# Hyena filter's spectrum computed ahead of the first feed-forward, and five modulation tiles multiplied by PE

## The reference

```python
mod = c_act @ w_ada[l] + b_ada[l]                   # nine vectors of 1024
(sh1, sc1, ga1, ...) = jnp.split(mod, N_MOD, axis=-1)
h = modulate(rms_norm(x, g_pre_ff1[l]), sh1, sc1)   # needs sh1 and sc1
f = swiglu(h, w1_gate[l], w1_up[l], w1_down[l])     # the first feed-forward
...
def hyena_filter_spectra(t, z, ...):                # for the fifth stage
    h = jnp.sin(sin_freq[0] * (z @ w1 + b1))
    h = jnp.sin(sin_freq[1] * (h @ w2 + b2))
    h = jnp.sin(sin_freq[2] * (h @ w3 + b3))
    h = (h @ w_out).reshape(L, HYENA_ORDER, 2, HYENA_WIDTH)
    h = h * jnp.exp(-t[:, None, None, None] * jnp.abs(decay))
    fwd, bwd = h[:, :, 0], h[:, :, 1]
    two = jnp.concatenate([fwd, zeros, bwd[:0:-1]], axis=0)
    two = two * lax.rsqrt(jnp.sum(two * two, axis=0, keepdims=True))
    return jnp.fft.rfft(two, axis=0)
```

## Time and profile before

| | us |
|---|---|
| median of 3 runs | 1576.78 (1573.79 to 1578.28) |
| the profiled execution | 1575.49 |
| its span | 1573.7 |
| PE busy | 1524.4 (97%) |
| DVE busy | 1023.6 (65%) |
| ACT busy | 758.5 (48%) |
| POOL busy | 222.7 (14%) |

### The profile page before, as it was taken

The page is one execution under the profiler, slowest core; times in us unless marked ns, Lnnn a source line. Parts: engine busy times, 40 slices in busy tenths (PEclk is TensorE's granted clock), DMA queues, the critical chain, the costliest instruction groups (busy, mean ns, idle before and its releaser), DMA issues.

```text
span 1573.7 us, 28410 instructions
## 1 busy us (share of the span) xinstructions
PE 1524.4 (97%) x10512; PEld 1401.8 (89%) x10512; DVE 1023.6 (65%) x1391; ACT 758.5 (48%) x1205; POOL 222.7 (14%) x255
## 2 busy tenths in 40 slices
PE   5989999999999998999999999999999999999997
PEld 5989999989988888999997899999999999899996
DVE  6998778766665456655567765556655569565554
ACT  2444645576456345444454344445444457454442
POOL 1596095311001011000000000000000000000000
PEclk9999999999999999999999999999999999999999
DMA  9888874236665455655543365554655544255551
GB/s 349 320 299 279 315 266 130 79 108 199 203 224 186 168 188 209 225 189 175 196 132 96 110 227 170 194 185 136 212 188 189 174 156 137 68 200 191 171 198 40
DMA packets 80563, 294.35 MB, mean 187 GB/s; under 512 B 9051, under 2 KB 9404, under 8 KB 79916
## 3 DMA queue, kind: packets, MB, share of 16 engines
q1 hardware_dynamic: 75728, 274.97, 50.8%
q0 software_dynamic: 3984, 16.21, 3.1%
q10 hardware_dynamic: 780, 2.18, 0.5%
HBM read 289.13 MB, written 3.15 MB: 186 GB/s over the span
## 4 chain that ended last, share of the span: by engine, by line
PE 84%; DVE 8%; ACT 3%; issue 2%; DMA 1%; POOL 1%; SPq 0%; DVEq 0%; ACTq 0%
PE bank L207 74%; DVE w_lo L191 3%; DVE arena L843 2%; PE bank L431 1%; PE bank L2033 1%; PE bank L2022 1%; PE bank L1273 1%; DMA arena<-ada 1%; PE bank L2409 1%; PE bank L2387 1%; ACT arena L308 1%; PE bank L424 1%; ACT w_hi L185 0%; PE bank L1259 0%; POOL stat L349 0%
## 5 line engine op out<-in xcount | busy, mean ns | idle before, releaser
L207 PE MATMUL bank<-h_hi,w_hi 128*128 128x256 f32 x2344 | 674.4, 288 | 5.8 <-DVE w_lo L191 4.4
L207 PE MATMUL bank<-h_lo,w_hi 128*128 128x256 f32 x2344 | 664.7, 284 | 0.0
L207 PE MATMUL bank<-h_hi,w_lo 128*128 128x256 f32 x2344 | 664.5, 283 | 0.0
L191 DVE TENSOR_TENSOR w_lo<-raw,w_hi 128x1024 fp32r<-128x1024 f32 x454 | 548.4, 1257 | 109.0 <-ACT w_hi L185 108.3
L185 ACT ACTIVATE w_hi<-raw 128x1024 fp32r<-128x1024 f32 x458 | 457.9, 1050 | 55.0 <-DMA raw<-panels 28.8
L207 PEld LDWEIGHTS bank<-h_hi,w_hi 128*128 128x128 f32 x2344 | 450.7, 192 | 21.0 <-issue 6.8
L207 PEld LDWEIGHTS bank<-h_lo,w_hi 128*128 128x128 f32 x2344 | 450.9, 192 | 5.7 <-issue 1.9
L207 PEld LDWEIGHTS bank<-h_hi,w_lo 128*128 128x128 f32 x2344 | 450.7, 192 | 0.0
L668 DVE TENSOR_TENSOR arena<-arena,bank 128x256 f32<-128x256 f32 x132 | 55.3, 419 | 253.7 <-PE bank L207 180.7
L207 PE MATMUL bank<-w_hi,f_hi 128*128 128x512 f32 x528 | 207.8, 394 | 1.6 <-DVE f_lo L673 1.4
L207 PE MATMUL bank<-w_hi,f_lo 128*128 128x512 f32 x528 | 206.9, 392 | 0.0
(11 more groups left out here) (329 smaller groups left out, 1387.2 us busy)
## 6 DMA issues: line engine op xcount, KB each, us to landing
raw<-panels SPq DMA_DIRECT2D x458, 512.0 KB, 4.6
arena<-ada SPq DMA_DIRECT2D x64, 512.0 KB, 5.2
arena<-ada POOLq DMA_DIRECT2D x8, 512.0 KB, 3.9
arena<-rows POOLq DMA_DIRECT2D x4, 512.0 KB, 4.6
spectrum<-arena POOLq DMA_DIRECT2D x2, 1024.0 KB, 7.9
arena<-spectrum POOLq DMA_DIRECT2D x1, 2048.0 KB, 18.0
X<-x_in SPq DMA_DIRECT2D x1, 1024.0 KB, 6.7
arena<-decay ACTq DMA_DIRECT2D x2, 512.0 KB, 5.6
```

The lines of the kernel that those rows point to most:

```text
L191: dve.tensor_tensor(w_lo[:, slot, :], raw[:, slot, :], w_hi[:, slot, :].bitcast(F32), ALU.subtract).then_inc(lo_ready, 1)
L207: last = pe.matmul(out_ap, a, b, start=start and n == 0, stop=stop and n == 2)
```

## The change

The spectrum's work leaves the second feed-forward. All three layers, the taps of both orders and the transform of order 0 go ahead of the first feed-forward, between the modulation's tiles. The transform of order 1 goes behind the first product of the first feed-forward (tile 0), and its sum behind `up(1)`; both sit in PE's list, and ACT's evictions of that transform sit between panels 2 and 3. Its five loads are issued by ACT's queue as soon as the small columns have landed, before ACT computes silu(c). Of the 16 modulation tiles PE multiplies 1, 3, 5, 9 and 11 (`ada_tile_pe`, one matmul per column block into bank 3, on top of which `ada_first_pe` adds DVE's sums), and SP waits for them by a semaphore of their own. The two `keep_busy` runs shrink from 24 and 10 matmuls to 6 and 10. POOL's list takes the even parts and squares ahead of `ada_middle_pool`, and the stores behind it; it waits for the stores' landing before `tables_pool`. Some buffers and PSUM banks move.

```diff
@@ -545,8 +548,15 @@
                     down(2, i)
 
             norm_pe(pe, at, first_up)
+            if n == 0:
+                for f in range(2):
+                    spectrum_rows_pe(pe, 1, f)
             up(1)
+            if n == 0:
+                filter_sums_pe(pe, 1)
             down(0, start=True)
+            if n == 0:
+                pe.wait_ge(filter_sums, 2)
             if n == 0:
...
@@ -573,8 +583,6 @@
                 for f in range(2, FT - 2):
                     up(f)
                     down(f - 1)
-                    piece_pe(pe, f)
-                pe.wait_ge(filter_sums, 2)
                 gate_pe(pe, 2, acc_gate_2, (6, 7))
...
                     act_panels(act, base + 3 * f + 2, 3)
-                    piece_first_act(act, f - 1)
                     hidden(f)
-                    piece_act(act, order, f - 1)
...
@@ -692,6 +696,7 @@
             dve_panels(dve, base + 5, 3)
             if n == 0:
                 params_rest_dve(dve, order)
+                filter_sums_dve(dve, 1)
             hidden(1)
...
                     dve_panels(dve, base + 3 * f + 2, 3)
-                    piece_dve(dve, order, f - 1)
...
         def ada_add(dve, a, dst):
 
             slot, k = a % ADA_RING, a % KT
+            tiles = 2 if a + 1 in BY_PE else 1
             dve.wait_ge(ada_loaded[slot], 16 * (a // ADA_RING + 1))
             if k == 0:
                 dve.tensor_scalar(dst, ada_ring[:, slot, :], c_act[:, 0:1], None,
-                                  ALU.mult).then_inc(ada_used, 1)
+                                  ALU.mult).then_inc(ada_used, tiles)
             else:
-                ada_multiply_add(dve, a, dst, ada_ring[:, slot, :], c_act[:, k:k + 1])
+                ada_multiply_add(dve, a, dst, ada_ring[:, slot, :], c_act[:, k:k + 1], tiles)
+
+        def ada_zero_pe(pe):
+
+            pe.wait_ge(const_ready, 3)
+            pe.matmul(bank[3][:, 0:2 * KT], ones[:, :], zero_cols, start=True, stop=False, skip_group_check=True)
+
+        def ada_tile_pe(pe, a):
+
+            slot, k, c = a % ADA_RING, a % KT, a // KT
+            pe.wait_ge(c_ready, 1)
+            pe.wait_ge(ada_loaded[slot], 16 * (a // ADA_RING + 1))
+            for j in range(KT):
+                mm = pe.matmul(bank[3][:, 8 * c + j:8 * c + j + 1], ada_ring[:, slot, j * P:(j + 1) * P],
+                               c_act[:, k:k + 1], start=False, stop=False, skip_group_check=True)
+            mm.then_inc(ada_by_pe, 1)
...
-        def ada_first_pe(pe):
-            for c in range(2):
-                pe.wait_ge(ada_used, 8 * c + 8)
-                sum_columns(pe, acc0[:, c, :], 3, 8 * c).then_inc(column_sums, 1)
-                keep_busy(pe, 1, (24, 10)[c])
+        def ada_first_pe(pe, c):
+
+            pe.wait_ge(ada_used, 8 * c + 8)
+            for j in range(KT):
+                mm = pe.matmul(bank[3][:, 8 * c + j:8 * c + j + 1], acc0[:, c, j * P:(j + 1) * P], ones[:, 0:1],
+                               start=False, stop=True, skip_group_check=True)
+            mm.then_inc(column_sums, 1)
...
             start_gate(pool, order, acc_gate_2, 2)
-            for i in range(5):
+            for i in range(KT):
                 load_late(pool, i)
-            even(pool, 0)
-            add_squares(pool, order, 0)
-            load_late(pool, 5)
-            store(pool, 0)
-            load_late(pool, 6)
-            even(pool, 1)
-            load_late(pool, 7)
-            add_squares(pool, order, 1)
-            store(pool, 1)
+
+        def spectrum_pool(pool, order):
+
+            for o in range(2):
+                even(pool, o)
+                add_squares(pool, order, o)
+            pool.wait_ge(squares_added, 2)
+            ada_middle_pool(pool, order)
+            for o in range(2):
+                store(pool, o)
             pool.wait_ge(filter_sums, 2)
             for o in range(2):
                 f = filter_scale[:, 4 * o:4 * o + 4]
                 pool.tensor_tensor(f, f, stat[:, MINUS_HALF:MINUS_HALF + 4], ALU.pow).then_inc(filter_scaled, 1)
-
-
+            pool.wait_ge(spectrum_stored, 32)
...
-        LAYER_TILES = (2, 4, 6)
-        TAP_TILES = ((8, 9), (13, 14))
-        SUM_TILES = (15, 18)
-        DFT_TILES = ((11, 12), (16, 17))
...
         def taps_pe(pe, o, m):
             pe.wait_ge(mlp_sin, 3)
-            if m:
-                pe.wait_ge(taps_done, 4 * o + 2)
-            elif o:
+            pe.wait_ge(tables_loaded, 32)
+            if o or m:
+                pe.wait_ge(taps_done, 4 * o + 2 * m)
+            if o and m == 0:
                 pe.wait_ge(spec_done, 4)
+                pe.wait_ge(filter_sums, 1)
...
         def load_spectrum(act):
             act.dma_start(feat_t, feats).then_inc(spec_loaded, 16)
             act.dma_start(mlp_ws, mlp_w[:, 0:192]).then_inc(spec_loaded, 16)
-            act.dma_start(filter_out[0:64, :], mlp_w[:, 192:2240]).then_inc(spec_loaded, 16)
-            act.dma_start(dft[:, 0, :, :], pool_mats[4]).then_inc(spec_loaded, 16)
-            act.dma_start(dft[:, 1, :, :], pool_mats[5]).then_inc(spec_loaded, 16)
             load_decay(act, 0)
+            act.dma_start(filter_out[0:64, :], mlp_w[:, 192:2240]).then_inc(tables_loaded, 16)
+            act.dma_start(dft.rearrange("p i m t -> p i (m t)"),
+                          pool_mats[4:6].rearrange("i p m t -> p i (m t)")).then_inc(tables_loaded, 16)
...
@@ -2718,7 +2693,10 @@
             sp.dma_start(ident[:, :], tables[0]).then_inc(x_loaded, 16)
             sp.dma_start(X[:, :, :], x_in.rearrange("(m p) d -> p m d", p=P)).then_inc(x_loaded, 16)
             for a in range(ADA_FIRST):
+                if a - ADA_RING in BY_PE:
+                    sp.wait_ge(ada_by_pe, BY_PE.index(a - ADA_RING) + 1)
                 load_ada(a)
+            sp.wait_ge(ada_by_pe, len(BY_PE))
             for g in range(8):
...
@@ -2749,9 +2727,10 @@
             order = Order(pool, pool_order)
             pool.memset(ones[:, :], 1.0).then_inc(const_ready, 1)
             pool.memset(stat[:, MINUS_HALF:MINUS_HALF + 4], -0.5).then_inc(const_ready, 1)
-            pool.wait_ge(const_ready, 2)
+            pool.memset(zero_cols, 0.0).then_inc(const_ready, 1)
+            pool.wait_ge(const_ready, 3)
             norm_pool(pool, 0, order)
-            ada_middle_pool(pool, order)
+            spectrum_pool(pool, order)
             tables_pool(pool, order)
...
@@ -2778,12 +2757,28 @@
         def _(act):
             order = Order(act, act_order)
             act.wait_ge(small_loaded, 16)
+            load_spectrum(act)
             act.activation(c_act, col("c", 0, 8), ACT.Silu).then_inc(c_ready, 1)
+            layer_act(act, 0)
             norm_act_squares(act, 0)
+            for layer in (1, 2):
+                layer_act(act, layer)
+            magnitudes_act(act, order, 0)
+            decay_factors_act(act, 0)
+            for m in range(MT):
+                tap_squares_act(act, 0, m)
+            magnitudes_act(act, order, 1)
+            decay_factors_act(act, 1)
+            for f in range(2):
+                spectrum_rows_act(act, 0, f)
             act_panels(act, 0, 2)
             act.wait_ge(mods_done, 1)
             norm_act_rest(act, 0)
             act_panels(act, 2, 1)
+            for m in range(MT):
+                tap_squares_act(act, 1, m)
+            for f in range(2):
+                spectrum_rows_act(act, 1, f)
...
-            for a in range(ADA_FIRST):
-                ada_add(dve, a, acc0[:, a // KT, :])
-                if a == 4:
-                    diag_dve(dve, 0)
+            def add_tiles(*tiles):
+                for a in tiles:
+                    ada_add(dve, a, acc0[:, a // KT, :])
+
+            layer_dve(dve, order, 0)
+            add_tiles(0)
+            layer_dve(dve, order, 1)
+            add_tiles(2)
+            layer_dve(dve, order, 2)
+            add_tiles(4)
+            taps_dve(dve, order, 0, 0)
+            add_tiles(6)
+            diag_dve(dve, 0)
+            taps_dve(dve, order, 0, 1)
+            odd_dve(dve, 0)
+            add_tiles(7, 8, 10, 12)
+            filter_sums_dve(dve, 0)
+            taps_dve(dve, order, 1, 0)
+            add_tiles(13)
+            taps_dve(dve, order, 1, 1)
+            add_tiles(14, 15)
             dve_panels(dve, 0, 1)
             ada_first_dve(dve, order)
             dve_panels(dve, 1, 1)
             low_dve(dve, 0, order)
+            odd_dve(dve, 1)
             dve_panels(dve, 2, 1)
...
@@ -2834,8 +2847,27 @@
         @block.tensor
         def _(pe):
             pe.wait_ge(const_ready, 2)
+            ada_zero_pe(pe)
+            layer_pe(pe, 0)
+            ada_tile_pe(pe, 1)
+            layer_pe(pe, 1)
+            ada_tile_pe(pe, 3)
+            layer_pe(pe, 2)
+            ada_tile_pe(pe, 5)
+            taps_pe(pe, 0, 0)
+            taps_pe(pe, 0, 1)
             norm_turn_pe(pe, 0)
-            ada_first_pe(pe)
+            for f in range(2):
```

(10 more changed lines are left out.)

95 lines of the change are left out of this document (27 added, 68 removed).

## The result

The changed kernel takes 1601.26 us (median of 4 runs, 1599.94 to 1601.77), the kernel before beside it 1575.28: a ratio of 1.0162 (95% interval 1.0145 to 1.0179), slower by 26 us. The forecast of 1586.8 had the sign right and the size wrong: the time measured lies beside that of rival C (1603), outside the range given. The profiled execution took 1601.77 us with a span of 1599.9, against 1575.49 and 1573.7 before.

What follows compares the result with a forecast made beforehand. PE bounds the second feed-forward; DVE and full DMA engines bound the start. +25.2 (modulation), +10.1 (first feed-forward's start) and -24.65 (second feed-forward) gave +10.6, taken as +10: 1586.8 us against the median, range 1581 to 1594.

Steps and rivals of the forecast that it cites:

- rival C: Start: PE stays at its slow pace, doubling its work from 34.0 to 51.1 us; +26, or 1603 us; chance 12%.
- Part 1: Second feed-forward: PE alone bounds it, so removing the spectrum's matmuls saves 24.65 us.
- Part 2: Start: the modulation ends later through the new lists, +23.6 us, or +25.2 with PE's slow start.
- a PE that starts from rest: Start, path up to 28 us: slow early PE work costs 1.6 us, bounds 0 and 4.3.
- the head: Start of the first feed-forward: added transform and held panels make DVE about 10.1 us later, PE 14.4 late.
- a run of 17 us is almost without gaps: PE's work from 34.0 to 51.1 us: argued against it staying at slow pace there.
- Two smaller steps: Start: silu(c) done and layer 0 on DVE from 7.6 us; modulation tile 1 landed at 13.9 us.
- Part 3: First feed-forward's start: order 1's transform and ACT's evictions hold panels 3 and 4, making DVE 10.0 us later.
- the difference of 4.3 is paid from PE's 4.41 idle us before 118: First feed-forward: PE's lateness beyond DVE's, 14.4 against 10.1 us, is absorbed by idle gaps and costs nothing.
- A: Start: DVE's work alone sets it, +5.9 us there; whole kernel -8.7, or 1568 us; chance 10%.
- B: First feed-forward's start: ACT's evictions don't hold panels 3 and 4; whole kernel +0.8, or 1578 us; chance 10%.
- PE at half pace after 34 us: Start: a listed sign that would show the forecast wrong.

Runs made afterwards that it cites:

- e11_relaid_fill: Changed kernel's spectrum work laid out anew, all modulation tiles on DVE, fillers in PE's waits, first column sum later: 1572.77 us, 0.9983 of the kernel before.
- e9_feats_first: Changed kernel with feature, layer and decay loads issued first on ACT and the two large tables' loads behind the first sine: 1599.56 us.
- e4_head: Changed kernel with ACT's evictions of order 1's transform moved behind the first silu and rounding of the first feed-forward: 1594.32 us.
- e13_copy_early: Changed kernel with DVE's copy of order 1's filter sum moved ahead of its chain of small instructions: 1596.18 us.
- e14_halved: Changed kernel with half the products of PE's layers, taps, five modulation tiles and second column sum left out at the start: 1588.56 us.
- e16_halved_copy: Changed kernel with PE's slow start pieces cut to half their work and DVE's copy of order 1's filter sum moved earlier: 1583.77 us.
- e1_fill: Changed kernel with keep_busy filler products added to PE's list at the start: 1600.27 us.
- e5: Kernel before with the filter's spectrum left out on every engine and constants stored in its place: 1546.05 us.
- e6b: Kernel before with order 1's transform moved from the second feed-forward's loop to behind its last product: 1570.30 us.
- e3: Kernel before with only the five modulation tiles moved to PE, the spectrum staying in the second feed-forward: 1582.20 us.

## Why the prediction was wrong, step by step

**Part 1 was right**: PE's pieces were the path, and nothing else came due. -24.65 measured -26.2, short by the longer panel product behind each piece.

**Part 2: the list was right, the pace was not.** The step that failed is "to this I add what a PE that starts from rest costs ... I take 1.6", with its bound of 4.3. It took the half pace for something of the first 28 us only, and too small even there. In the chain above ten pieces exceed their durations at full pace: four tiles by 1.86, 1.82, 0.62 and 1.82, four halves of taps by 1.81, 1.84, 1.80 and 1.81, a layer by 0.47, and the turn by 1.49 (it takes 3.84 in `e11_relaid_fill`). That is 15.3 us, and with the column sum behind them (1.9) 17.2. Of the 15.3, 9.3 stand ahead of 41 us, where PE had not come to its full pace yet and the forecast had 1.6 and a bound of 4.3; 6.1 stand behind the fall at 52 us, where it had nothing. Halving the pieces took 10.9 off the modulation's end. Rival C had this mechanism, though its 1603 is near the measured time in part by luck: it doubled all work from 34.0 to 51.1 us, +16.5, where the transforms and the first column sum ran at full pace and 1.5 + 6.1 us were lost; what it lacked came from pieces ahead of that stretch and from the lateness in the head. I gave it 12% with the argument that "a run of 17 us is almost without gaps": without gaps it was, yet it is in this run that the clock fell. I had read the clock row as a matter of idle time and did not ask what PE does in its busy rows; the five tiles put 40 more products of one column (80 records) on it.

The same trace held a warning that I did not follow up: the granted clock reads 0.94 over the start of the kernel before, so it falls there for a few microseconds too.

Two smaller steps cancelled. Layer 0 started on DVE at 11.45, not 7.6, since the features and the layers' weights had landed only at 10.2; with their loads issued first they were there by 5.5 (`e9_feats_first`). Tile 1 was there by 11.2, not 13.9. The same run shows that this matters little, as tile and layer alternate in PE's list.

**Part 3: the hold-up by ACT's list was right** (`e4_head`: 5 to 7 us of time, 9.1 at the first `f_lo`). The head was +12.3 for +10.1. The difference is the column sum at half pace, 3.58: in `e13_copy_early`, where it took 1.95, the head is (93.30 - 68.11) - 14.89 = +10.3, and in `e14_halved`, where half of it took 1.05, (82.28 - 57.78) - 14.89 = +9.6.

**The step "the difference of 4.3 is paid from PE's 4.41 idle us before 118" failed.** PE's new wait of 7.59 ahead of `up(2)` made it later than DVE by more than the gaps could pay, and 3.9 us came due. `e13_copy_early` removes them by moving one copy.

With these two put right the sum holds within 1 us or so: `e16_halved_copy` gives +8.8 to +9.4. That it fits so well is partly luck, as the second feed-forward and the rest gave back 2.5 us more than was put (27.2 in its trace), and the modulation, at +26.3, took 1.1 of it.

**The other rivals.** A (DVE alone sets the start) needed PE ahead everywhere; DVE waited for PE 7.2, 3.6, 4.4, 4.2 and 3.2 us. B's mechanism, panels not held, is refuted by the 9.86 us wait. Of the list of what would show it wrong, the last item, "PE at half pace after 34 us", is what came.

By the Trainium skill, page "TensorE: Matmul & The Clock Gate", section "What's actually happening", the gate goes by "how busy the PE has been recently". By the profile's busy share the trace disagrees: PE was busy 2.00 of 2.00 us in each row from 48 to 54 and fell to half. What helps the reader is to look at what stands in the busy rows.

## What to carry to other kernels

Before work is moved onto an engine that is idle for a third of a stretch, price it at the pace that the engine has there, from rows of that stretch, and not from rows of a stretch in which it runs full; the same matmuls cost twice as much here. Where a list in strict order gets new work ahead of something that others wait for (evictions ahead of panels, a copy behind a chain), moving one item is worth microseconds: 5 to 7 and 4 to 5 here. And time given back by a bound engine (26 us) bought next to nothing where the work landed in a start that is a chain over four engines, a ratio of 0.9983 in the best layout; putting 7 us of it into an existing idle place at a stage's boundary did pay, 4 us.

## What the runs showed of the hardware

- At the start the granted clock reads 1.00 while matmuls go at half pace: taps take 3.78 us at 26.5 us in the changed kernel, and 1.98 at 28.2 in `e1_fill`, both under a reading of 1.00. In `e14_halved`, where PE writes constants early, the reading is 0.50 from 10 to 34 us, and the pieces are no slower than with a reading of 1.00. So the duration of a known piece tells the pace, the reading at a kernel's start does not.
- A half pace once reached could last: 0.50 from 54 to 76 us in the changed kernel, with PE busy for most of it on tiles, taps, a column sum and fillers. But its length varied: in `e13_copy_early`, whose list is the same there, the reading was back at 1.00 in the row from 68, fell again to 0.59 and 0.55 in the rows from 70 to 74, and the second column sum took 1.95 us for 3.58.
- The first product of a stream behind a piece of another shape costs extra: 1.6 us over the 13 pieces of the spectrum, some 0.12 each. In the trace of the kernel before, the first product behind taps starts at 456.07 and the next 0.22 us later, those after it 0.12 apart.
- The start of one and the same list varied from kernel to kernel: the first modulation tile landed at 9.78, 8.63, 8.85 and 8.51 us in the traces of before, `e5`, `e6b` and `e3`.
